# Expert weights fetched in runs of 16 KB per partition, one transfer and one semaphore a weight

## The reference, cut to what matters

```python
pg = softmax(xt @ rg_w + rg_b); g_sel = argmax(pg)          # 1 of 4 groups
le_sel = logits of the 8 experts of that group
top_v, top_i = top_k(softmax(le_sel), 2)                     # 2 of 8 experts
for gi in range(4):                                          # all 32 experts
    h = silu(xt @ e_wg[gi]) * (xt @ e_wu[gi])                # 1024 -> 512
    out = out + (h * comb) @ e_wd[gi]                        # 512 -> 1024
```

## Time and profile before

| | before |
|---|---|
| median of 3 runs | 1391.08 us |
| traced execution: time, span | 1391.12 us, 1389.3 us |
| PE busy | 1217.5 us (88%) |
| DVE, ACT, POOL busy | 30%, 24%, 7% |
| DMA packets, bytes | 131170, 283.97 MB |
| weight transfers | 192 of 1 MB |
| gather into `xg`, issue to landing | 6.9 us median, 32 of them |

### The profile page before, as it was taken

How to read it: one execution, slowest core, us unless ns; L and a number is a source line. 1 busy time by engine, 2 the same in 40 slices (tenths; PEclk the granted TensorE clock), 3 DMA queues, 4 the chain that set the end, 5 groups by cost and what they waited for, 6 DMA issues and landing times.

```text
span 1389.3 us, 23984 instructions
## 1 busy us (share of the span) xinstructions
PE 1217.5 (88%) x10668; PEld 898.0 (65%) x10668; DVE 413.7 (30%) x709; ACT 327.2 (24%) x546; POOL 98.6 (7%) x141
## 2 busy tenths in 40 slices
PE   4999999999988989999999998987887888778880
PEld 4899998986778778999999877332333333233330
DVE  4337622344162254233343314101111110000115
ACT  5444322332222244222232313100000000000102
POOL 3000000000000000000000001311111111111110
PEclk8999999998999899999999999999999999999995
DMA  7110104001122463233233837999999999999976
GB/s 222 61 31 1 33 6 154 4 3 35 61 65 91 110 184 115 70 91 88 73 92 90 320 124 289 340 395 413 411 412 412 412 412 413 412 413 411 408 289 211
DMA packets 131170, 283.97 MB, mean 204 GB/s; under 512 B 25011, under 2 KB 72325, under 8 KB 122874
## 3 DMA queue, kind: packets, MB, share of 16 engines
q1 hardware_dynamic: 124970, 270.60, 53.3%
q0 software_dynamic: 5440, 9.46, 1.8%
q10 hardware_dynamic: 656, 2.36, 0.4%
HBM read 274.11 MB, written 15.61 MB: 209 GB/s over the span
## 4 chain that ended last, share of the span: by engine, by line
PE 63%; DMA 21%; DVE 7%; issue 3%; ACT 2%; POOL 2%; SPq 1%; POOLq 0%; DVEq 0%; ACTq 0%
DMA slot<-in_e_wu_dram 13%; PE bank L1285 8%; DMA xg<-normed_tokens,il 7%; PE bank L631 7%; PE bank L1244 6%; PE bank L1246 6%; PE bank L1245 6%; PE bank L624 3%; PE bank L1394 2%; PE bank L1395 2%; PE bank L1396 2%; PE bank L1458 2%; PE bank L1462 2%; PE bank L750 1%; PE bank L1460 1%
## 5 line engine op out<-in xcount | busy, mean ns | idle before, releaser
L624 PE MATMUL bank<-slot,xs 128*64 128x512 f32 x512 | 244.6, 628 | 57.4 <-DMA slot<-in_e_wu_dram 56.2
L625 PE MATMUL bank<-slot,xs 128*64 128x512 f32 x512 | 245.7, 630 | 0.0
L624 PEld LDWEIGHTS bank<-slot,xs 128*64 128x64 f32 x512 | 69.2, 143 | 197.7 <-issue 196.0
L1244 PE MATMUL bank<-xnh,wh 128*128 128x256 f32 (+1 forms) x448 | 133.5, 298 | 0.5 <-ACT bt_ogm L2151 0.5
L1245 PE MATMUL bank<-xnl,wh 128*128 128x256 f32 (+1 forms) x448 | 133.3, 297 | 0.0
L1246 PE MATMUL bank<-xnh,low 128*128 128x256 f32 (+1 forms) x448 | 133.2, 297 | 0.0
L631 PE MATMUL bank<-slot,ht 128*64 128x512 f32 x512 | 123.3, 626 | 0.5 <-DVE ht L933 0.5
L2243 DVE TENSOR_TENSOR low<-ring,wh 128x1536 fp32r<-128x1536 f32 (+1 forms) x45 | 90.0, 2005 | 101.4 <-ACT wh L1914 94.4
L819 ACT ACTIVATE sg<-bank 64x512 f32<-64x512 f32 x32 | 19.0, 594 | 416.3 <-PE bank L625 416.3
L923 DVE TENSOR_TENSOR h<-sg,bank 64x512 f32<-64x512 f32 x32 | 21.7, 680 | 313.7 <-ACT sg L819 292.4
L1914 ACT ACTIVATE wh<-ring 128x1536 fp32r<-128x1536 f32 (+1 forms) x45 | 75.4, 1680 | 49.1 <-PE bank L1285 31.4
(11 more groups left out here) (469 smaller groups left out, 2316.5 us busy)
## 6 DMA issues: line engine op xcount, KB each, us to landing
slot<-in_e_wg_dram SPq DMA_DIRECT2D x64, 1024.0 KB, 21.5
slot<-in_e_wu_dram SPq DMA_DIRECT2D x64, 1024.0 KB, 22.0
slot<-in_e_wd_dram SPq DMA_DIRECT2D x64, 1024.0 KB, 19.3
ring<-in_w_in_dram SPq DMA_DIRECT2D x13, 1024.0 KB, 8.8
ring<-in_w_in_dram SPq DMA_DIRECT2D x24, 512.0 KB, 4.3
ring<-in_w_branch_dram SPq DMA_DIRECT2D x24, 256.0 KB, 4.8
kvs<-in_cache_mem_k_dram SPq DMA_DIRECT2D x8, 512.0 KB, 5.0
kvs<-in_cache_mem_v_dram SPq DMA_DIRECT2D x8, 512.0 KB, 4.2
```

Source lines behind the costliest of these rows:

```text
L624: pe.matmul(out[64:128, :], tok, wg[:, FF * k:FF * k + FF], start=(k == 0), stop=(k == KD - 1))
L625: mm = pe.matmul(out[0:64, :], tok, wu[:, FF * k:FF * k + FF], start=(k == 0), stop=(k == KD - 1))
L1244: pe.matmul(part, w_h, xh_(k, cols), start=(k == 0), stop=False)
```

## The change

The weights are laid out so that partition `p` holds eight neighbouring rows of `e_wg` and `e_wu` (four of `e_wd`): one run of 16 KB. A weight is one transfer of 2 MB with one semaphore. The gate and up loads of expert `e` both wait for `("gu", e - 3)`, the half step `("gh", ...)` frees nothing any more. `gate_up` waits for both whole weights before its first matmul, `down` for the whole down weight. Partition `q` now stands for features `8q` to `8q + 7`, so the tokens are turned by `turn_tokens`: for each of eight chunks and each half of the partitions one product of a 64x64 block (every eighth column of `xg`) with a 64x64 identity, 16 products instead of four transposes. `turn_h` takes every fourth column instead of every second, with as many instructions. The general path is changed likewise and is left out here.

```diff
@@ -379,7 +379,7 @@
         assert cu <= z + 16384
 
         xg = [sb(f"xg{n}", [128, 512], F32, at) for n, at in enumerate((z + 23040, z + 16384))]
-        xs = [sb(f"xs{n}", [128, 4, 128], F32, z3 + 40960 + 2048 * n) for n in range(2)]
+        xs = [sb(f"xs{n}", [128, KD, CAP], F32, z3 + 40960 + 2048 * n) for n in range(2)]
         sg = sb("sg", [CAP, FF], F32, z3 + 45056)
         h2 = sb("h2", [CAP, FF], F32, z3 + 47104)
         ht = [sb(f"ht{n}", [128, 4, CAP], F32, z3 + 49152 + 1024 * n) for n in range(2)]
@@ -532,7 +532,7 @@
 
         g2_loaded, wr_loaded, x2_stored, far_stored, listed = (sem(n) for n in ("g2_loaded", "wr_loaded", "x2_stored", "far_stored", "listed"))
         tab_loaded, fg_loaded = sem("tab_loaded"), sem("fg_loaded")
-        eslot_loaded = [[sem(f"eslot{n}_half{f}_loaded") for f in range(2)] for n in range(NSLOT)]
+        eslot_loaded = [sem(f"eslot{n}_loaded") for n in range(NSLOT)]
         gathered = [sem("gathered0"), sem("gathered1")]
         scattered = [sem("scattered0"), sem("scattered1")]
         yb_loaded = [[sem(f"yb{t}_{k}_loaded") for k in range(2)] for t in range(5)]
@@ -560,16 +560,14 @@
         act_f = Steps(sem("act_f"), [x for t in range(5) for x in (("sq", t), ("root", t))])
         dve_f = Steps(sem("dve_f"), ["clear", ("sum", 0)] + [x for t in range(1, 5) for x in (("sum", t), ("inverse", t - 1), ("y", t - 1))]
                       + [("inverse", 4), ("y", 4)])
-        wgu = [w[0].rearrange("g e (k p c) f -> (g e) p k (c f)", k=4, c=2) for w in (e_wg, e_wu)]
-        wdn = e_wd[0].rearrange("g e (k p c) d -> (g e) p k (c d)", k=2, c=2)
+        wgu = [w[0].rearrange("g e (p c) f -> (g e) p (c f)", c=KD) for w in (e_wg, e_wu)]
+        wdn = e_wd[0].rearrange("g e (p c) d -> (g e) p (c d)", c=4)
 
         def moe_sp(sp):
 
-            def load(e, n, halves=(0, 1)):
-                slot, k = (3 * e + n) % NSLOT, 2 if n < 2 else 1
-                for f in halves:
-                    sp.dma_start(slots[slot][:, 2048 * f:2048 * f + 2048].rearrange("p (k n) -> p k n", k=k),
-                                 (wgu[n] if n < 2 else wdn)[e][:, k * f:k * f + k, :]).then_inc(eslot_loaded[slot][f], 16)
+            def load(e, n):
+                slot = (3 * e + n) % NSLOT
+                sp.dma_start(slots[slot][:, :], (wgu[n] if n < 2 else wdn)[e]).then_inc(eslot_loaded[slot], 16)
 
             for n in range(3):
                 load(0, n)
@@ -588,10 +586,9 @@
                 sp.wait_ge(gathered[n], 16)
             load(2, 2)
             for e in range(3, EX):
-                for f in range(2):
-                    pe_m.wait(sp, ("gu" if f else "gh", e - 3))
-                    load(e, 0, (f,))
-                    load(e, 1, (f,))
+                pe_m.wait(sp, ("gu", e - 3))
+                load(e, 0)
+                load(e, 1)
                 pe_m.wait(sp, ("d", e - 3))
                 load(e, 2)
                 if e == 5:
@@ -618,9 +615,15 @@
             for _ in range(n):
                 pe.matmul(psum[bank][:, 0:128], ones[:, :], before[:, :], start=True, stop=True)
 
+        def turn_tokens(pe, rows_):
+            for c in range(KD):
+                for p in (0, 64):
+                    mm = pe.matmul(psum[2][p:p + 64, CAP * c:CAP * c + CAP], rows_[p:p + 64, c:512:KD], i64[p:p + 64, :], start=True, stop=True)
+            return mm
+
         def expert_in(pe, out, x, wg, wu, part=range(KD)):
             for k in part:
-                tok = x[:, k % 4, 64 * (k // 4):64 * (k // 4) + 64]
+                tok = x[:, k, :]
                 pe.matmul(out[64:128, :], tok, wg[:, FF * k:FF * k + FF], start=(k == 0), stop=(k == KD - 1))
                 mm = pe.matmul(out[0:64, :], tok, wu[:, FF * k:FF * k + FF], start=(k == 0), stop=(k == KD - 1))
             return mm
@@ -746,17 +749,15 @@
 
             def turn_in(e):
                 pe.wait_ge(gathered[e % 2], 16 * (e // 2 + 1))
-                for c in range(4):
-                    mm = pe.transpose(psum[2][:, 128 * c:128 * c + 128], xg[e % 2][:, 256 * (c // 2) + c % 2:256 * (c // 2) + 256:2], ident[:, :])
-                pe_m.done(mm, ("t", e))
+                pe_m.done(turn_tokens(pe, xg[e % 2]), ("t", e))
 
             def gate_up(e):
                 act_e.wait(pe, ("xs", e))
                 if e >= 2:
                     dve_e.wait(pe, ("h", e - 2))
+                for n in range(2):
+                    pe.wait_ge(eslot_loaded[(3 * e + n) % NSLOT], 16 * ((3 * e + n) // NSLOT + 1))
                 for f in range(2):
-                    for n in range(2):
-                        pe.wait_ge(eslot_loaded[(3 * e + n) % NSLOT][f], 16 * ((3 * e + n) // NSLOT + 1))
                     mm = expert_in(pe, psum[e % 2], xs[e % 2], slots[3 * e % NSLOT], slots[(3 * e + 1) % NSLOT], range(4 * f, 4 * f + 4))
                     pe_m.done(mm, ("gu" if f else "gh", e))
 
@@ -764,17 +765,15 @@
                 dve_e.wait(pe, ("ht", e))
                 if e >= 2:
                     dve_e.wait(pe, ("y", e - 2))
-                for f in range(2):
-                    pe.wait_ge(eslot_loaded[(3 * e + 2) % NSLOT][f], 16 * ((3 * e + 2) // NSLOT + 1))
-                    mm = expert_out(pe, psum[4 + e % 2], ht[e % 2], slots[(3 * e + 2) % NSLOT], range(2 * f, 2 * f + 2))
-                pe_m.done(mm, ("d", e))
+                pe.wait_ge(eslot_loaded[(3 * e + 2) % NSLOT], 16 * ((3 * e + 2) // NSLOT + 1))
+                pe_m.done(expert_out(pe, psum[4 + e % 2], ht[e % 2], slots[(3 * e + 2) % NSLOT]), ("d", e))
 
             def turn_h(e):
                 dve_e.wait(pe, ("h", e))
                 if e >= 1:
                     dve_e.wait(pe, ("ht", e - 1))
                 for f in range(4):
-                    mm = pe.transpose(psum[3][:, CAP * f:CAP * f + CAP], h2[:, 256 * (f // 2) + f % 2:256 * (f // 2) + 256:2], ident[0:CAP, 0:CAP])
+                    mm = pe.transpose(psum[3][:, CAP * f:CAP * f + CAP], h2[:, f:512:4], ident[0:CAP, 0:CAP])
                 pe_m.done(mm, ("ht", e))
 
             turn_in(0)
@@ -809,7 +808,7 @@
                 pe_m.wait(act, ("t", e))
                 if e >= 2:
                     pe_m.wait(act, ("gu", e - 2))
-                act_e.done(act.activation(xs[e % 2][:, :, :], psum[2][:, :].rearrange("p (c n) -> p c n", n=128), ACT.Copy), ("xs", e))
+                act_e.done(act.activation(xs[e % 2][:, :, :], psum[2][:, :].rearrange("p (c n) -> p c n", n=CAP), ACT.Copy), ("xs", e))
 
             evacuate(0)
             for e in range(EX):
...
```

More of the change, by code:

```diff
@@ L1025, in general_sp @@
                     for n in range(3):
-                        src = (wgu[n] if n < 2 else wdn)[bass.ds(e, 1)].rearrange("a p k f -> (a p) k f")
-                        sp.dma_start(slots[n][:, :].rearrange("p (k n) -> p k n", k=4 if n < 2 else 2), src).then_inc(more_loaded, 16)
+                        src = (wgu[n] if n < 2 else wdn)[bass.ds(e, 1)].rearrange("a p f -> (a p) f")
+                        sp.dma_start(slots[n][:, :], src).then_inc(more_loaded, 16)
                     pe_n.wait(sp, "y", MORE * e + (MORE - 1))
@@ L1037, in general_pe @@
                         await_round(pe, more_gathered, 16 * r + 16)
-                        for c in range(4):
-                            mm = pe.transpose(psum[2][:, 128 * c:128 * c + 128], xg[0][:, 256 * (c // 2) + c % 2:256 * (c // 2) + 256:2], ident[:, :])
-                        pe_n.done(mm, "t")
+                        pe_n.done(turn_tokens(pe, xg[0]), "t")
                         await_round(pe, more_loaded, 48 * e + 48)
@@ L1057, in general_act @@
                         pe_n.wait(act, "t", r)
-                        act_n.done(act.activation(xs[0][:, :, :], psum[2][:, :].rearrange("p (c n) -> p c n", n=128), ACT.Copy), "xs")
+                        act_n.done(act.activation(xs[0][:, :, :], psum[2][:, :].rearrange("p (c n) -> p c n", n=CAP), ACT.Copy), "xs")
                         pe_n.wait(act, "gu", r)
```

## The result

Before, 1390.3 us (four runs, 1388.8 to 1396.1); after, 1530.9 us (four runs, 1528.5 to 1534.1); ratio 1.100, 95% interval 1.098 to 1.102. The traced execution has a span of 1532.4 us, 143 us longer than before, and a mean TensorE clock of 0.904 against 0.951.

What follows compares the result with a forecast made beforehand. From the first scatter on the loop bounds: 7.27 + 9.5 + 0.85 = 17.6 us a round, above the stream's 15.41 us. The stage takes 523.4 us, 52 us more; added to 1391.1 us, 1443 us, range 1414 to 1480 us.

Steps and rivals of the forecast that it cites:

- the loop: Expert stage: down, copy to `yo`, scatter, gather of expert e + 3, turning, next down; forecast to bound at 17.6 us a round.
- part 2: Gathers beside 16 KB packets: landing 9.5 us instead of 6.85 us, and low clock in down costing 0.85 us a round.
- part 3: Turning the tokens by 16 products of 64x64 instead of four transposes: 0 us, between -0.1 and +0.6 us.
- Part 1: Weight stream in 16 KB runs: 15.41 us an expert instead of 15.97 us, removing 16 us from the stream.
- the reading of two thirds of the packets waiting: Gather queue: of 10 packets an engine some 7 wait for one weight packet each, 153 ns longer, giving 1.14 us.
- The rule of turns packet by packet: DMA engines take turns between queues, a whole packet at a time; taken strictly, the gather takes 10.9 us.
- Part 4: Whole weights: later loads cost nothing; 3.45 us lost at the last `gate_up` if the stream bounds, 0 with the loop.
- (d): Rival, the loop: all ten packets wait, down nearly always at low clock; 19.9 us a round, 1510 us; chance 0.06.
- (a): Rival: the gather is not lengthened and the stream stays the bound; 1378.5 us, faster; chance 0.12.
- (b): Rival: the weights' runs are cut again to 8 KB, gather 7.4 us; 1385 us; chance 0.04.
- (c): Rival: packets whole but only part of the step shows, gather 7.8 to 8.1 us; within 5 us of before; chance 0.05.

## Why the prediction was right in direction and wrong in size

Forecast 1443 us, measured 1531 us, outside the range. Slower, and for the reason given: PE waits for `xg` before every turning, never for weights; the scatters keep one pitch from beginning to end; the gathers stand in the chain. Opening the loop took back 137 of the 140 us. The size failed in three terms of the round:

| term of a round | forecast | measured | what shows it |
|---|---|---|---|
| gather in flight | 9.5 us | 10.2 us | the chain after; median 10.1 us |
| turning beyond 0.72 us | 0 (up to 0.6) | 1.47 us | 2.19 us in the chain after |
| down beyond 3.63 us | 0.85 us | 1.6 us | 5.22 us in the chain after |
| round | 17.6 us | 20.3 to 20.5 us | scatters, chain |

29 x (20.3 - 17.6) = 78 us of the 88 us missing. Another 15.5 us are the later first scatter, where the forecast had no change: 8 us are the standstill, 3 x 1.47 = 4.4 us the first turnings, and gate and up behind the standstill run their first six pairs of instructions at the low clock, 5.17 us in place of 2.6. That is 6 us too much: the 29th round took only 14.6 us, 5.7 less than the others where the forecast had 3 less, and the traced execution was 3.2 us above the median.

Two steps of the prediction failed, and the experiment with the old turning in the kernel after tells what each is worth. There the turning takes 1.10 us in the chain, 0.4 us more than before and near the forecast of 0, and the time is 1501.9 us: 59 of the 88 us are there without the new turning. They come from part 2, most of it from the share of rounds with down at the low clock. The other 29 us come with the new turning, 11 in the rounds and 17.6 before the first scatter, the standstill of open cause among them, and belong to part 3.

**Part 1 (rate) held.** With the loop opened the stream ran at 425 GB/s, 3.2% above 412; the forecast of 15.41 for 15.97 us is 3.6%. A 16 KB packet takes 611 ns in the median of the trace after, forecast 622 ns.

**Part 2 (gathers and the clock behind them) held in kind and failed in size.** 10.1 us lies between the 9.5 us taken and the bound of 10.9 us. The three points are 6.9, 7.4 and 10.1 us for 4, 8 and 16 KB packets: the step from 8 to 16 KB is 2.7 us, not twice a step of 1.1 us. The 7.42 us taken for 8 KB came from one gather; the landings with 8 KB alone have their median at 7.4 us, against 6.9 us with 4 KB, so the first step is 0.5 us and not 1.14, and the reading of two thirds of the packets waiting was not a law. What does set it stays open. The rule of turns packet by packet (the Trainium skill, "DMA: Bandwidth & Descriptors", section "Queues, rings and completion order"), with one packet of the trace taken as one turn, gave 10.9 us, 0.8 us above the median, where my reduction of it lies 0.6 us below. A packet of that page holds several descriptors, so that reading of it is not shown. The share of rounds with a low clock was the larger miss of this part: I took one in two, it was nearly every one (29 of the last 31 downs take over 4 us), at 1.6 us of the 1.7 us known from the earlier trace rows. With the old turning it was 28 of 31, and down takes 5.92 us in the chain, 2.3 us above full clock where 0.85 was taken. PE's waits are 5.4 us in the mean from 950 to 1340 us; the forecast had 4.7 us and kept the clock's share at a half.

**Part 3 (turning at nothing) failed in its count.** The price was taken from products whose starts stood in pairs 0.06 us apart, and 16 products were counted as 16 instructions; such a pair is one product's two instructions. The line of the earlier trace rows stands for 64 products (8 for each of 8 chunks), and the trace before has 128 instructions there. The page after counts 1024 for 512 products: a float32 product of this form is two instructions on PE, a transpose is one (x4 for four). 32 x 0.068 us = 2.19 us. Even my upper bound, +0.6 us, rested on 16. The doubling could be read before the run: the earlier trace rows show a down as x16, and its code (`expert_out`) has 4 x 2 = 8 products (the 16 matmuls told for `down` above are instructions). And the turning doesn't only last longer: right behind a wait it leaves the clock low for down. Alone in the kernel before it cost 51 us, 17.0 us a round against 14.6 to 16, plus the standstill at the start.

The two overlap, so what each costs depends on the order. With 16 KB packets the wait of 5 to 6 us brings the clock down by itself, so the old turning saves only 0.4 us a round there; with 4 KB packets the turning alone made the difference. The turning first: turning in the kernel before +51 us; whole weights and layout with 4 KB packets -4 us, within spread; 8 KB packets +7 us; from 8 to 16 KB another +86 us. The turning last: everything else +111 us, the turning +29 us.

**Part 4 (whole weights) held within the noise**: with the loop as the bound -4 us together with the layout, within spread, forecast 0; where the stream bounds about 5 us (2 to 8), forecast 3.45 us.

**The rivals.** (d), 19.9 us a round and 1510 us at a chance of 0.06, was nearest; it had the gather too long (10.9 us), the low clock right, and no turning. It describes the experiment with the old turning well: 19.9 us a round, 1501.9 us. (a), (b) and (c) fell: the gathers lengthened, the packets weren't cut, and the step wasn't partial.

## What to carry to other kernels

Before a bulk stream is made of longer packets, look whether a small transfer on another queue stands on a loop: here 13 GB/s more for the stream made each gather 3 us longer, and the loop that it stood on took over ten times the gain. Open the loop first (here a few lines of issue order, worth nothing by themselves in the kernel before), then lengthen the packets. And count the instructions that a product becomes in the trace, by type, before pricing it from another row: what stands right behind a wait is paid for again in the clock of all that follows.

## What the runs showed of the hardware that was not expected

- A gather (scatter and gather of a round are 160 small packets on their queue) lands in 6.9 us beside 4 KB packets of another queue, in 7.4 us beside 8 KB, in 10.1 us beside 16 KB. The step is not in proportion.
- A float32 product of 64x64 is two instructions, and the clock hardly changes their pitch: 16 products took 2.07 us at full clock, 0.065 us an instruction, and 2.19 us at 0.50, 0.068 us; 32 products of 128x128 are 64 instructions, 7.34 us.
- PE after 2.3 us of waiting still showed 1.00, fell within 2.2 us of small products (0.87) and left the next 5 us at 0.72; after 5 to 6 us of waiting it began at 0.50.
- Where the stream bounds, it moves 412 GB/s with runs of 4 and 8 KB, 419 GB/s with 8 KB alone and 425 GB/s with 16 KB.
- From 1100 to 1165 us SP takes 1.9 to 8.1 us for each issue of a 2 MB weight in runs of 4 and 8 KB (the experiment with whole weights), and 0.3 to 0.4 us in runs of 16 KB (the kernel after, and with the early gather).
- A standstill of 8 us with no releaser in the trace comes and goes with small edits to PE's program.
